# Where the causal mask of a state-space stage is added: by TensorE in PSUM, or by VectorE in the subtraction that follows

## The chip, the core and the metric

The kernel runs on one core of a Trainium2 chip. The metric is the device time of one execution in microseconds (us). Lower is better. The core has five engines that run their own instruction streams and meet at semaphores: TensorE (PE, matrix products from SBUF into PSUM), VectorE (DVE), ScalarE (ACT), GpSimd (POOL), and SyncE (SP), which here issues the transfers of the weights.

## What is computed

Two stacks of two layers each, on 512 tokens of width 1024 in fp32. The layers of the second stack have three branches: a Mamba-2 state-space branch, sliding-window attention and forgetting attention. The change lies in the first. Its core in the reference, for each of 16 heads (4 groups of 4) and each of 4 chunks of 128 tokens:

```
a_cum = jnp.cumsum(a_dt, axis=-1)
causal = idx[:, None] >= idx[None, :]
seg = a_cum[..., :, None] - a_cum[..., None, :]
decay = jnp.where(causal, jnp.exp(jnp.where(causal, seg, 0.0)), 0.0)
cb = jnp.einsum('bclgn,bcsgn->bgcls', cc, bc)
y_diag = jnp.einsum('bgrcls,bcsgrp->bclgrp', cb[:, :, None] * decay, x_dt)
...
y_off = jnp.einsum('bclgn,bcgrpn,bgrcl->bclgrp', cc, prev, jnp.exp(a_cum))
return (y_diag + y_off)
```

The kernel gets the zeros of `decay` by adding -1e30 above the diagonal (`NEG` in `consts()`) before the exponential.

## The kernel before

Weights come in 264 waves of 1 MB. SyncE loads a wave into one of two buffers, GpSimd splits it into a high and a low fp32r part (`split_wave`, L320 and L325), and TensorE makes three products for each of its tiles (high by high, low by high, high by low: L357, L358, L359 in `tile_product`). Activations are split in the same way. Nearly all TensorE time goes into these products.

No scheduler orders the work. Each engine's stream is written out by hand, and engines wait for counts of named semaphores (`s("seg")`, `s("decayed")`, ...). An engine stands at a wait until it is met, with all that is behind it.

The state-space stage is `ssm(g, first)` on TensorE and the loop over `GROUPS` (4) on VectorE and ScalarE, in each of the two layers of the second stack: 8 rounds. One group is 4 heads, r = 0 to 3. Its last part, for which these names stand:

- `rows(r)`, TensorE: a matmul L704 spreads the cumulated log-decays of head r over all partitions, 512 columns (4 chunks of 128), into bank 4 + r % 2; then four matmuls L706 of the identity with the mask add the mask to each chunk of 128 columns. The last one counts up `seg`.
- `segments(r)`, VectorE: L1745 subtracts the column of head r (its log-decays down the partitions, one value for each partition and chunk), from PSUM into `dm` (printed as merged), and counts up `seg_read`.
- ScalarE: L1155 takes the exponential of `dm` in place, and counts up `seg_exp`.
- `decay(r)`, VectorE: L1754 multiplies by `cbs`, the products of C and B, and counts up `decayed`.
- `within(r)`, TensorE: four matmuls L718 with x. `across(t)`: L724, the part from the states of earlier chunks, for two heads at a time.
- `output(t)`, VectorE: L1758, L1760 and L1762 put both parts together and count up `y_read`.
- `fill(n)`, TensorE: n times three products of the group's last waves, put between the rest so that TensorE has work while the others are busy.

The order on the two engines that matter:

```
TensorE: rows(0) rows(1) fill(6) within(0) rows(2) fill(3) within(1) across(0) rows(3) fill(4) within(2) within(3) across(1) fill(1)
VectorE: segments(0) segments(1) decay(0) segments(2) decay(1) L1772 output(0) segments(3) decay(2) decay(3) output(1)
```

`rows(r)` for r of 2 and 3 waits until `segments(r - 2)` has read the bank. `segments(r)` for r of 2 and 3 waits for `within(r - 2)`, since `dm` has two halves. `within(2)` also waits for `output(0)`, which reads the bank it writes. Ahead of `segments(0)` VectorE builds the states (L1729, L1734, L1736) from TensorE's L695.

`own` (class `Steps`) is a semaphore with which VectorE waits for its own operations: `own(ins)` counts one, `own.done()` waits until all that were counted have ended. At the start of the program VectorE casts the identity and the mask to fp32r (L1418, L1420), and TensorE waits for both (`s_setup`) ahead of the first attention heads.

Of the kernel before, what the change touches and what calls it, by code (L numbers as in the profile page):

```python
# [22 lines left out]
F32R = mybir.dt.float32r  # L23
I32 = mybir.dt.int32
ALU = mybir.AluOpType
# [3 lines left out]
P = 128  # L29
# [4 lines left out]
QB = S // P  # L34
# [23 lines left out]
C_MT, C_WM1, C_WM2 = 464, 592, 1104  # L58
# [91 lines left out]
def program(nc, weights, par1, par2, const, x_in, out, NWAVES=NWAVES):  # L150
    ctx = ExitStack()
    with ctx:
        def sb(name, shape, dt=F32, stack=ctx):
            return stack.enter_context(nc.sbuf_tensor(name, shape, dt))

        def sem(name):
            return ctx.enter_context(nc.semaphore(name))

        psum = ctx.enter_context(nc.psum_tensor("banks", [P, 8, S], F32))

        def bank(n, m=1):
            return psum[:, n:n + m, :] if m > 1 else psum[:, n, :]
# [12 lines left out]
        cst = sb("cst", [P, C_MT])  # L175
        rot = sb("rot", [P, 2, S])
        par = sb("par", [P, 160])
        identr = sb("identr", [P, P], F32R)
        seg_mask = sb("seg_mask", [P, P], F32R)
        wide_mask = sb("wide_mask", [P, C_C1 - C_WM2])  # L180
        nsink = sb("nsink", [P, 64])
        rstd = sb("rstd", [P, 16])
# [2 lines left out]
        ident = cst[:, C_ID:C_ID + P]  # L185
# [9 lines left out]
        ylo = sb("ylo", [P, KT, S], F32R, big)  # L195
        merged = sb("merged", [P, KT, S], F32, big)
        sg = sb("sg", [P, KT, S], F32, big)
        mask_in = sg[:, 0, 0:P]
        t1 = ExitStack()
        pb = [sb(f"pb{i}", [P, 2, 16 + S], F32, t1) for i in range(3)]  # L200
        pfix = sb("pfix", [P, 2, 16], F32, t1)
# [17 lines left out]
        cum = sb("cum", [P, 2, S], F32R, second)  # L219
        sel = sb("sel", [P, 4, P], F32R, second)  # L220
        selp = sb("selp", [P, 2 * P], F32R, second)
        cols = sb("cols", [P, 2, QB, 16], F32, second)
# [32 lines left out]
        dm = merged[:, 6:8, :]  # L255
# [7 lines left out]

        s_x, s_const = sem("s_x"), sem("s_const")
        s_masks, s_tables = sem("s_masks"), sem("s_tables")
        s_setup = sem("s_setup")
        s_par = sem("s_par")
        s_par_free = sem("s_par_free")
        raw_full = [sem(f"raw_full{i}") for i in range(2)]
# [7 lines left out]
        def s(name):  # L277
            if name not in sems:
                sems[name] = sem(name)
            return sems[name]  # L280
# [11 lines left out]
        @block.sync  # L292
        def _(sp):
            sp.dma_start(x[:, :, :], x_in).then_inc(s_x, 16)
            sp.dma_start(cst[:, :], const[:, 0:C_MT]).then_inc(s_const, 16)
            sp.dma_start(mask_in, const[:, C_MT:C_WM1]).then_inc(s_masks, 16)
            for p in range(2):
                sp.dma_start(raw[p][:, :], weights[p]).then_inc(raw_full[p], 16)
            sp.dma_start(rot[:, :, :], const[:, C_C1:C_C2].rearrange("p (a n) -> p a n", a=2)).then_inc(s_tables, 16)
            sp.dma_start(wide_mask[:, 0:S], const[:, C_WM1:C_WM2]).then_inc(s_tables, 16)  # L300
            with sp.Fori(1, NWAVES // 2) as j:
                for p in range(2):

                    sp.wait_ge(split, 2 * j + p - 1)
                    sp.dma_start(raw[p][:, :], weights[2 * j + p]).then_inc(raw_full[p], 16)
            sp.wait_ge(s("x_done"), 1)
            sp.dma_start(out, merged[:, :, :]).then_inc(s("stored"), 16)
            sp.wait_ge(s("stored"), 16)
# [35 lines left out]
        def _(pe):  # L344
# [104 lines left out]
            with pe.Fori(0, DEPTH) as L:  # L449
# [7 lines left out]
                for g in range(4):  # L457
# [3 lines left out]
                    for f in range(2):  # L461
                        mm = tile_product(bank(4 + 2 * (g % 2) + f), 0, g * 4 + f * 2, yhi, ylo, (2 * g, 2 * g + 1))
                    mm.then_inc(s("pool_done"), 1)
                pe.wait_ge(s("pool_read"), 4 * L + 4)
                mm = pe.matmul(psum[:, 4, 0:2], ones, lamc[:, 0:2], start=True, stop=True)
                mm.then_inc(wave_done, 1)

                pe.wait_ge(s_setup, 2)

                def tail(it, step):  # L470
                    if step == 0:
# [143 lines left out]
            with pe.Fori(0, DEPTH) as L:  # L615
                base = L * N2 + DEPTH * N1
                norm_spread(L + 2 * DEPTH)
                for p in range(2):

                    start_wave(base + p, p)  # L620
                    for k in range(KT):
                        if p == 0:
                            normed(L + 2 * DEPTH)(k)
                        mm = tile_product(bank(2 * p), p, k, xhi, xlo, [k], start=k == 0, stop=k == KT - 1)
# [27 lines left out]
                def ssm(g, first):  # L652
                    it = L * GROUPS + g
                    n = base + 4 * g + W_SSM
# [18 lines left out]
                    for t in range(3):  # L673
                        if t:
                            mm = fill((3, 5)[t - 1])
# [3 lines left out]
                        for c in range(QB):  # L679
                            mm = pe.transpose(psum[:, 7 - t, c * P:(c + 1) * P], cv[:, t, c * P:(c + 1) * P], ident)  # L680
                        mm.then_inc(s("ssm_turned"), 1)
                    pe.wait_ge(s("conv"), 4 * it + 4)
                    for c in range(QB):
                        mm = pe.matmul(psum[:, 4, c * P:(c + 1) * P], cv[:, 2, c * P:(c + 1) * P], cv[:, 3, c * P:(c + 1) * P],
                                       start=True, stop=True)
# [4 lines left out]
                    for t in range(2):  # L690
                        mm = pe.matmul(bank(4 + t), selp[:, t * P:(t + 1) * P], cum[:, 0, :], start=True, stop=True)
                    mm.then_inc(s("decay_rows"), 1)
                    pe.wait_ge(s("xdt"), it + 1)
                    for c in range(3):
                        mm = pe.matmul(psum[:, 6 + c // 2, (c % 2) * 256:(c % 2) * 256 + 256], btok[:, c, :], xd2[:, c, :],  # L695
                                       start=True, stop=True)
                    mm.then_inc(s("states"), 1)

                    def rows(r):
                        if r == 0:  # L700
                            pe.wait_ge(s("decay_out"), it + 1)
                        if r >= 2:
                            pe.wait_ge(s("seg_read"), 4 * it + r - 1)
                        pe.matmul(bank(4 + r % 2), sel[:, r, :], cum[:, 0, :], start=True, stop=False)  # L704
                        for c in range(QB):
                            mm = pe.matmul(psum[:, 4 + r % 2, c * P:(c + 1) * P], identr[:, :], seg_mask[:, :],  # L706
                                           start=False, stop=c == QB - 1)
                        mm.then_inc(s("seg"), 1)

                    def within(r):  # L710
                        if r == 0:
# [10 lines left out]
                    def across(t):  # L722
# [3 lines left out]
                        mm.then_inc(s("y_across"), 1)  # L726

                    rows(0)
                    rows(1)
                    fill(6)  # L730
                    within(0)
# [114 lines left out]
                for k in range(SWA_STEPS):  # L846
                    g, m = divmod(k, SWA_PAIRS)
# [3 lines left out]
                    def fill(first, last):  # L851
                        for i in SWA_FILL[k]:
                            cs = [c for j, c in products[first:last] if j == i]
                            if cs:
                                swa_fill(i, cs[0], cs[-1] + 1)
# [108 lines left out]
                for k in range(STEPS):  # L964
                    g, m = divmod(k, PAIRS)
# [386 lines left out]
        def _(dve):  # L1352
            own = Steps(dve, dve_own, apart)
# [61 lines left out]
            for i in range(4):  # L1415
                add_squares(0, i, IN_ORDER)
            dve.wait_ge(s_const, 16)
            dve.tensor_copy(identr[:, :], ident).then_inc(s_setup, 1)  # L1418
            dve.wait_ge(s_masks, 16)
            dve.tensor_copy(seg_mask[:, :], mask_in).then_inc(s_setup, 1)  # L1420
            with dve.Fori(0, DEPTH) as L:
                base = L * N1
                dve.wait_ge(s_par, 16 * (L + 1))
# [35 lines left out]
                for g in range(4):  # L1459
# [7 lines left out]
                    for t in range(2):  # L1467
                        c = P_PS + 2 * g + t
# [140 lines left out]
            with dve.Fori(0, DEPTH) as L:  # L1609
# [63 lines left out]
                with dve.Fori(0, GROUPS) as g:  # L1673
                    it = L * GROUPS + g
                    n = base + 4 * g + W_SSM
# [65 lines left out]
                    def segments(r):  # L1741
                        dve.wait_ge(s("seg"), 4 * it + r + 1)
                        if r >= 2:
                            dve.wait_ge(s("y_within"), 4 * it + r - 1)
                        dve.tensor_tensor(dm[:, r % 2, :].rearrange("p (c n) -> p c n", c=QB),  # L1745
                                          psum[:, 4 + r % 2, :].rearrange("p (c n) -> p c n", c=QB),
                                          cols[:, 1, :, bass.ds(4 * g + r, 1)].to_broadcast([P, QB, P]),
                                          ALU.subtract).then_inc(s("seg_read"), 1)

                    def decay(r):  # L1750
                        dve.wait_ge(s("seg_exp"), 4 * it + r + 1)
# [129 lines left out]
                for k in range(SWA_STEPS):  # L1881
                    g, m = divmod(k, SWA_PAIRS)
# [66 lines left out]
                for k in range(STEPS):  # L1949
                    g, m = divmod(k, PAIRS)  # L1950
# [220 lines left out]
```

## Time and profile before

| | |
|---|---|
| median of 3 timed runs | 3625.15 us (3624.57 to 3625.71) |
| profiled execution, its own time | 3621.37 us |
| its span, first to last instruction | 3619.5 us |
| TensorE busy, granted clock | 3457.3 us (96%), 0.983 |
| VectorE, ScalarE, GpSimd busy | 1471.9 (41%), 816.5 (23%), 2124.9 us (59%) |
| mask matmuls L706 | 128 in all |
| `segments` L1745 | 32, of 688 ns |

The profile is one execution as the hardware profiler recorded it. Times within it count from its first instruction. A matmul's record lasts longer than the time for which it holds TensorE (the pipeline overlaps the next one: wave products of 390 ns start 0.23 us apart), so what a matmul costs is read from the distance of two starts, or from the chain of waits, where the pieces follow each other without overlap. "L12" is line 12 of the kernel before. An engine name with a q (DVEq) is that engine's queue of small instructions: address computations and waits.

### The profile page before, as it was taken

How to read it: one execution, taken by the hardware profiler on the slowest of the kernel's cores; microseconds unless marked ns; L12 is line 12 of the kernel's file. 1: busy time of each engine (PE TensorE's matmuls, PEld its weight loads, DVE VectorE, ACT ScalarE, POOL GpSimd, SP SyncE). 2: the span in 40 equal slices, each digit the busy share in tenths (PEclk: the TensorE clock that was granted, in tenths of full speed). 3: DMA queues.
4: the chain of work that ended last, by engine and by line, in shares of the span. 5: the costliest groups of instructions: out<-in, count | busy, mean ns of one | idle time of the engine just before them, and what ended most of it. 6: DMA issues, size and time to landing. Idle time of an engine off the chain costs nothing.

```text
span 3619.5 us, 49401 instructions
## 1 busy us (share of the span) xinstructions
PE 3457.3 (96%) x17270; PEld 2766.4 (76%) x17270; DVE 1471.9 (41%) x2814; ACT 816.5 (23%) x1659; POOL 2124.9 (59%) x2116
## 2 busy tenths in 40 slices
PE   8999899998999899999999999999899999999998
PEld 6778688887777688877877777777778777777776
DVE  4545322104555321116664652332366545523323
ACT  1223111001233111002222540332122225413320
POOL 6745567766555477665556556445756475464454
PEclk9999999999999999999999999999999999999998
DMA  3211122222211122231212212111212122121121
GB/s 129 83 68 70 62 88 94 93 101 75 82 62 66 70 93 93 94 115 59 81 68 83 71 70 94 60 70 70 95 68 74 68 84 79 72 82 70 59 70 70
DMA packets 39930, 285.38 MB, mean 79 GB/s; under 512 B 4688, under 2 KB 5200, under 8 KB 5728
## 3 DMA queue, kind: packets, MB, share of 16 engines
q1 hardware_dynamic: 38880, 282.13, 21.5%
q8 instruction: 104, 1.70, 0.2%
q10 hardware_dynamic: 896, 1.14, 0.1%
q14 instruction: 50, 0.41, 0.0%
HBM read 281.15 MB, written 2.10 MB: 78 GB/s over the span
## 4 chain that ended last, share of the span: by engine, by line
PE 83%; DVE 8%; issue 4%; ACT 3%; POOL 1%; DMA 0%; DVEq 0%; ACTq 0%; POOLq 0%
PE banks L357 20%; PE banks L359 19%; PE banks L358 19%; PE banks L596 2%; PE banks L595 2%; PE banks L594 2%; PE banks L909 1%; PE banks L933 1%; PE banks L920 1%; PE banks L400 1%; PE banks L565 1%; PE banks L402 1%; PE banks L401 1%; PE banks L912 1%; PE banks L718 1%
## 5 line engine op out<-in xcount | busy, mean ns | idle before, releaser
L320 POOL TENSOR_SCALAR whi<-raw 128x512 fp32r<-128x512 f32 x1056 | 731.5, 702 | 1457.6 <-PE banks L359 1223.4
L325 POOL TENSOR_TENSOR wlo<-raw,whi 128x512 fp32r<-128x512 f32 x1056 | 1438.1, 1372 | 0.0
L357 PE MATMUL banks<-xhi,whi 128*128 128x512 f32 x2976 | 1220.6, 410 | 41.3 <-DVE xlo L1387 15.4
L359 PE MATMUL banks<-xhi,wlo 128*128 128x512 f32 x2976 | 1169.7, 393 | 0.0
L358 PE MATMUL banks<-xlo,whi 128*128 128x512 f32 x2976 | 1167.6, 392 | 0.0
L357 PEld LDWEIGHTS banks<-xhi,whi 128*128 128x128 f32 x2976 | 564.2, 190 | 190.0 <-issue 33.3
L359 PEld LDWEIGHTS banks<-xhi,wlo 128*128 128x128 f32 x2976 | 562.9, 189 | 123.9
L358 PEld LDWEIGHTS banks<-xlo,whi 128*128 128x128 f32 x2976 | 565.1, 190 | 109.6 <-issue 6.7
L357 PE MATMUL banks<-yhi,whi 128*128 128x512 f32 x544 | 217.5, 400 | 17.0 <-DVE ylo L1557 5.6
L358 PE MATMUL banks<-ylo,whi 128*128 128x512 f32 x544 | 214.0, 393 | 0.0
L359 PE MATMUL banks<-yhi,wlo 128*128 128x512 f32 x544 | 213.7, 393 | 0.0
L1919 DVE CUSTOM_DVE_ANT_0 banks<-banks,wide_mask 128x128 f32<-128x128 f32 (+3 forms) x128 | 63.4, 495 | 262.9 <-PE banks L912 262.9
L1585 DVE SCALAR_TENSOR_TENSOR hg<-hg,banks 128x512 f32<-128x512 f32 x44 | 30.2, 687 | 335.2 <-ACT hg L1094 335.2
L1294 ACT ACTIVATE work<-banks,st 128x128 f32<-128x128 f32 (+3 forms) x128 | 67.5, 528 | 322.7 <-PE banks L920 320.9
L594 PE MATMUL banks<-hhi,whi 128*128 (+1 forms) x352 | 136.9, 389 | 0.0
L595 PE MATMUL banks<-hlo,whi 128*128 (+1 forms) x352 | 136.9, 389 | 0.0
L596 PE MATMUL banks<-hhi,wlo 128*128 (+1 forms) x352 | 136.9, 389 | 0.0
L357 PEld LDWEIGHTS banks<-yhi,whi 128*128 128x128 f32 x544 | 103.5, 190 | 43.7 <-issue 8.9
L359 PEld LDWEIGHTS banks<-yhi,wlo 128*128 128x128 f32 x544 | 103.4, 190 | 22.0
L358 PEld LDWEIGHTS banks<-ylo,whi 128*128 128x128 f32 x544 | 103.3, 190 | 22.0 <-issue 1.0
L1094 ACT ACTIVATE hg<-banks 128x512 f32<-128x512 f32 x44 | 26.4, 599 | 348.2 <-PE banks L359 348.2
L1008 ACT ACTIVATE merged<-x 128x1024 f32<-128x1024 f32 x24 | 25.1, 1058 | 349.3 <-DVE x L1599 233.5
(260 smaller groups left out, 4260.0 us busy)
## 6 DMA issues: line engine op xcount, KB each, us to landing
raw<-weights SPq DMA_DIRECT2D x264, 1024.0 KB, 4.8
x<-x_in SPq DMA_DIRECT2D x1, 2048.0 KB, 8.2
out<-merged SPq DMA_DIRECT2D x1, 2048.0 KB, 6.3
rot<-const SPq DMA_DIRECT2D x1, 512.0 KB, 11.8
rot<-const ACTq DMA_DIRECT2D x1, 512.0 KB, 3.3
wide_mask<-const ACTq DMA_DIRECT2D x1, 384.0 KB, 4.1
wide_mask<-const SPq DMA_DIRECT2D x1, 256.0 KB, 12.5
cst<-const SPq DMA_DIRECT2D x1, 232.0 KB, 8.4
```

The source lines that it names most:

```text
L320: pool.tensor_scalar(whi[p][:, w], raw[p][:, w], 1.0, 1.0, ALU.mult, ALU.mult).then_inc(s("hi_written"), 1)
L325: return pool.tensor_tensor(wlo[p][:, w], raw[p][:, w], whi[p][:, w].bitcast(F32), ALU.subtract)
L357: pe.matmul(dst, whi[p][:, w], hi[:, k, :], start=start and i == 0, stop=False)
L358: pe.matmul(dst, whi[p][:, w], lo[:, k, :], start=False, stop=False)
L359: mm = pe.matmul(dst, wlo[p][:, w], hi[:, k, :], start=False, stop=stop and last_k)
L400: pe.matmul(dst, xhi[:, k, t], whi[p][:, w], start=k == 0, stop=False)
L401: pe.matmul(dst, xlo[:, k, t], whi[p][:, w], start=False, stop=False)
L594: pe.matmul(bank(f), whi[p][:, w], hhi[:, k0 + k2, :], start=start and k2 == 0, stop=False)
L595: pe.matmul(bank(f), whi[p][:, w], hlo[:, k0 + k2, :], start=False, stop=False)
L596: mm = pe.matmul(bank(f), wlo[p][:, w], hhi[:, k0 + k2, :], start=False, stop=stop and k2 == 1)
L1294: act.activation(pr2[:, u % 2, 0:w], psum[:, 4 + u % 3, 0:w], ACT.Exp, scale=-1.0, bias=st2[:, 1, c:c + 1], accum_out=st2[:, 2, c:c + 1]). ...
L1919: dve.tensor_tensor_reduce(sc, sc, blocked(w), -0.125, FAR, ALU.add, ALU.min, st2[:, 1, c:c + 1]).then_inc(s("fox_max"), 1)
```

## The change

TensorE's four identity matmuls of each `rows(r)` go, and `seg` is counted up by the spreading matmul. VectorE's one subtraction over 128x512 becomes four scalar_tensor_tensor over 128x128, one for each chunk: (PSUM - column) + mask, with the column as a [128, 1] scalar and the mask from SBUF. The first three are counted by `own`; the fourth waits for them and counts up `seg_read`. The mask stays in fp32 and is loaded straight to its place, the fp32r copy of the identity goes, and so do the two casts at the start and TensorE's wait for them.

```diff
-        identr = sb("identr", [P, P], F32R)
-        seg_mask = sb("seg_mask", [P, P], F32R)
+        seg_mask = sb("seg_mask", [P, P])
...
-        mask_in = sg[:, 0, 0:P]
...
-        s_setup = sem("s_setup")
...
-            sp.dma_start(mask_in, const[:, C_MT:C_WM1]).then_inc(s_masks, 16)
+            sp.dma_start(seg_mask[:, :], const[:, C_MT:C_WM1]).then_inc(s_masks, 16)
...
-                pe.wait_ge(s_setup, 2)
...
-                        pe.matmul(bank(4 + r % 2), sel[:, r, :], cum[:, 0, :], start=True, stop=False)
-                        for c in range(QB):
-                            mm = pe.matmul(psum[:, 4 + r % 2, c * P:(c + 1) * P], identr[:, :], seg_mask[:, :],
-                                           start=False, stop=c == QB - 1)
-                        mm.then_inc(s("seg"), 1)
+                        pe.matmul(bank(4 + r % 2), sel[:, r, :], cum[:, 0, :], start=True, stop=True).then_inc(s("seg"), 1)
...
             dve.wait_ge(s_const, 16)
-            dve.tensor_copy(identr[:, :], ident).then_inc(s_setup, 1)
             dve.wait_ge(s_masks, 16)
-            dve.tensor_copy(seg_mask[:, :], mask_in).then_inc(s_setup, 1)
...
-                        dve.tensor_tensor(dm[:, r % 2, :].rearrange("p (c n) -> p c n", c=QB),
-                                          psum[:, 4 + r % 2, :].rearrange("p (c n) -> p c n", c=QB),
-                                          cols[:, 1, :, bass.ds(4 * g + r, 1)].to_broadcast([P, QB, P]),
-                                          ALU.subtract).then_inc(s("seg_read"), 1)
+                        for c in range(QB):
+                            if c == QB - 1:
+                                own.done()
+                            ins = dve.scalar_tensor_tensor(dm[:, r % 2, c * P:(c + 1) * P], psum[:, 4 + r % 2, c * P:(c + 1) * P],
+                                                           cols[:, 1, c, bass.ds(4 * g + r, 1)], seg_mask[:, :],
+                                                           ALU.subtract, ALU.add)
+                            if c < QB - 1:
+                                own(ins)
+                            else:
+                                ins.then_inc(s("seg_read"), 1)
```

VectorE's stream from the last step of the states to `decay(0)`, before (ISA rows are queue instructions, here the computation of an address; merged is `dm`):

```order
L1734 TENSOR_TENSOR hst<-hst,banks 128x256 [waits dve_own]
L1745 ISA [waits dve_own,seg]
L1745 TENSOR_TENSOR merged<-banks,cols 128x512
L1745 ISA [waits seg]
L1745 TENSOR_TENSOR merged<-banks,cols 128x512
L1753 ISA [waits seg_exp]
L1754 TENSOR_TENSOR merged<-merged,cbs 128x512 [waits ssm_evac]
```

and now, where `segments` is L1738 and `decay` L1750; of the two `segments` the second stands here:

```order
L1738 ISA [waits seg]
L1738 SCALAR_TENSOR_TENSOR merged<-banks,cols,seg_mask 128x128
L1738 ISA
L1738 SCALAR_TENSOR_TENSOR merged<-banks,cols,seg_mask 128x128
L1738 ISA
L1738 SCALAR_TENSOR_TENSOR merged<-banks,cols,seg_mask 128x128
L1738 ISA [waits dve_own]
L1738 SCALAR_TENSOR_TENSOR merged<-banks,cols,seg_mask 128x128
L1749 ISA [waits seg_exp]
L1750 TENSOR_TENSOR merged<-merged,cbs 128x512 [waits ssm_evac]
```

The order of the steps is the same. Each of the four operations has its own address instruction, and that of the fourth stands behind the wait for the first three.

## Rows read from the trace of the kernel before

**Rows 1.** The page: busy time of the engines; shares of the chain that ended last.
```profile
PE 3457.3 (96%) x17270; PEld 2766.4 (76%) x17270; DVE 1471.9 (41%) x2814; ACT 816.5 (23%) x1659; POOL 2124.9 (59%) x2116
...
PE 83%; DVE 8%; issue 4%; ACT 3%; POOL 1%; DMA 0%; DVEq 0%; ACTq 0%; POOLq 0%
```

**Rows 2.** Chain of waits in the second group, `rows(0)`: start us, us, what.
```profile
1751.77 0.32 PE banks L704
1752.08 0.40 PE banks L706 x4
```

**Rows 3.** The same chain, from `across(0)` to `within(2)`.
```profile
1762.30 0.88 PE banks L724 x6
...
1763.21 0.06 DVEq L1758
...
1763.32 0.75 DVE ya L1758
...
1764.54 0.02 issue
...
1765.45 0.69 DVE merged L1745
...
1766.76 0.14 issue
1766.89 1.79 PE banks L718 x16
```

**Rows 4.** Who TensorE waited for: us in total, times, longest.
```profile
PE banks L718 <- DVE merged L1754: 2.3, 8, 0.3
```

**Rows 5.** Timeline of VectorE, second group: start us, us, instruction [idle before <-releaser].
```profile
1754.02 0.42 DVE L1734 TENSOR_TENSOR hst<-hst,banks 128x256 f32<-128x256 f32 x1
1754.69 1.29 DVE L1745 TENSOR_TENSOR merged<-banks,cols 128x512 f32<-128x512 f32 x2 [0.26 <-DVE hst L1734]
1756.18 0.69 DVE L1754 TENSOR_TENSOR merged<-merged,cbs 128x512 f32<-128x512 f32 x1 [0.21 <-ACT merged L1155]
1759.32 0.69 DVE L1745 TENSOR_TENSOR merged<-banks,cols 128x512 f32<-128x512 f32 x1 [2.45 <-PE banks L706]
1759.93 0.68 DVE L1754 TENSOR_TENSOR merged<-merged,cbs 128x512 f32<-128x512 f32 x1
...
1763.32 0.75 DVE L1758 SCALAR_TENSOR_TENSOR ya<-merged,par,banks 128x512 f32<-128x512 f32 x1 [1.58 <-PE banks L724]
1763.98 0.55 DVE L1760 TENSOR_TENSOR ea<-ea,banks 128x384 f32<-128x384 f32 x1
```

**Rows 6.** Timeline of TensorE, second group: `within(0)` and `within(1)`.
```profile
1757.26 1.09 PE L718 MATMUL banks<-merged 128*64 128x128 f32 x8
...
1761.21 1.09 PE L718 MATMUL banks<-merged 128*64 128x128 f32 x8
```

**Rows 7.** Groups of VectorE instructions by shape: busy us, mean ns | idle before.
```profile
L1919 DVE CUSTOM_DVE_ANT_0 banks<-banks,wide_mask 128x512 f32<-128x512 f32 x32 | 22.3, 696 | 60.5 <-PE banks L912 60.5
...
L1758 DVE SCALAR_TENSOR_TENSOR ya<-merged,par,banks 128x512 f32<-128x512 f32 x16 | 12.0, 747 | 29.9 <-PE banks L724 29.9
L1837 DVE CUSTOM_DVE_ANT_0 banks<-banks,wide_mask,nsink 128x128 f32<-128x128 f32 x32 | 11.5, 359 | 36.3 <-PE banks L803 28.2 <-DVE work L1850 7.4 <-DVE st L1837 0.8
...
L1919 DVE CUSTOM_DVE_ANT_0 banks<-banks,wide_mask 128x128 f32<-128x128 f32 x32 | 9.5, 296 | 97.5 <-PE banks L912 97.5
...
L1516 DVE CUSTOM_DVE_ANT_0 banks<-banks,wide_mask,rqs 128x128 f32<-128x128 f32 x16 | 5.5, 359 | 6.4 <-PE banks L533 6.4
```

**Rows 8.** Timeline of VectorE at the program's start, the first operation behind the casts.
```profile
17.88 0.17 DVE L1359 TENSOR_SCALAR banks<-banks 128x4 f32<-128x4 f32 x1 [2.44 <-PE banks L419]
```

**Rows 9.** Timeline of TensorE, two gaps in later stages.
```profile
1942.36 0.47 PE L357 MATMUL banks<-xhi,whi 128*128 128x512 f32 x1 [1.68 <-DVEq L1806]
...
1982.76 0.87 PE L814 MATMUL banks<-cst,work 128*128 128x128 f32 x3 [2.03 <-ACT work L1190]
```

**Rows 10.** Stretches around these gaps: us, PE busy (x), granted clock, DMA share, GB/s.
```profile
1982.80:1986.20 3.40, 3.40 (x11) 0.51 0.57 241
...
1940.00:1946.00 6.00, 4.33 (x20) 1.00 0.36 152
```

## The prediction

> **What bounds the kernel now.** I read the page first. TensorE is busy 96% of the span and holds 83% of the chain that ended last, VectorE 8% [rows 1]: as a whole TensorE is the bound, VectorE has spare time, and the change seems to move work from the full engine to one at 41%. That average says nothing of the stage that changes, so the sum is made there. The stage runs 8 times (4 groups in each of 2 layers). I read the chain of waits in the second group, then VectorE's and ScalarE's timelines there, and at last the prices of small VectorE operations.
>
> The chain shows that `rows` costs 0.32 + 0.40 us, 0.40 us of it the four mask matmuls of 128 columns [rows 2]. It also shows where TensorE does not set the pace: between `across(0)` and `within(2)` it runs through VectorE, from the end of L724 at 1763.18 through L1758, L1760, L1762, `segments(3)` (L1745) and `decay(2)` (L1754) to the matmuls L718 at 1766.89 [rows 3]. TensorE waits for L1754 in all 8 groups alike, 2.3 us in total and 0.3 at most [rows 4]. The other two hand-overs are nearly tight. The multiply of `decay(0)` starts at 1756.18 and that of `decay(1)` at 1759.93, 0.69 and 0.68 us long [rows 5]; with 0.14 us to the matmul [rows 3] they would release `within(0)` at 1757.01 and `within(1)` at 1760.75. TensorE reaches these at 1757.26 and 1761.21 (its L718 in [rows 6]). The slack is 0.25 and 0.46 us.
>
> **The removed matmuls.** 8 groups x 4 rows x 0.40 = 12.8 us of TensorE time. It counts only where no wait takes its place. `rows(0)` and `rows(1)` lie before `within(0)`, `rows(2)` before `within(1)`, and `rows(3)` runs beside the VectorE chain of [rows 3], so its 0.40 turns into waiting at once. Even if VectorE paid nothing more, `within(0)` could come only 0.25 earlier, since `decay(0)` waits for the exponential of `segments(0)`, which starts when VectorE has the states (L1734 ends 1754.44, L1745 starts 1754.69 [rows 5]). `within(1)` would then gain its 0.40, `within(2)` nothing: 0.65 us a group, **5.2 us at most** in all.
>
> **The price of four small operations.** Let T be the time from the start of a `segments` to the start of the operation behind it; now 0.61 (1759.32 to 1759.93 [rows 5]). The new form is four scalar_tensor_tensor of 128x128, from PSUM and `seg_mask`, with the column as a pointer scalar. No such row exists. The nearest is the custom operation of L1837 and L1516 (PSUM, an SBUF mask and a pointer scalar, 128x128): 359 ns. Without a pointer (L1919) it is 296, and at 512 columns 696; so 384 columns are worth 0.40 us and a pointer 0.06 [rows 7]. Scalar_tensor_tensor with a pointer takes 747 at 512 (L1758) [rows 7], less 0.40 is 0.35: I take **0.35**. It releases the engine earlier than it ends: L1758 starts at 1763.32, the next at 1763.98 [rows 5], 0.66, less 0.40 is **0.26**. The fourth waits until the third has ended and then computes its address: from L724's end at 1763.18 to L1758, the same pair of steps, 0.14 [rows 3]; its bounds are 0.02, a wait with no address (the issue between L1760 and L1762, rows 3), and 0.26, with one more queue step (L1734 to L1745, rows 5). So T = 0.26 + 0.26 + 0.35 + 0.14 + 0.26 = **1.27**. The low bound is the price without a pointer: 0.20 + 0.20 + 0.30 + 0.02 + 0.20 = 0.92. The high one lets nothing overlap and takes 359: 4 x 0.36 + 0.26 = 1.70. By the sum below these ends are worth 0 and 23.9 us. The addresses of the second and third (0.06 each on the queue, as for L1758 in rows 3) fit under 0.26.
>
> The Trainium skill (VectorE: DVE Perf Modes, The TRN2 errata) gives PSUM to SBUF 120 cycles plus one per column at 0.96 GHz, 258 ns at 128 columns. As an estimate by that page, with the overlap of 0.09 and the wait of 0.14, T would be 0.17 + 0.17 + 0.26 + 0.14 + 0.17 = 0.91 and the change free. The trace disagrees for operands like these: 296 without and 359 with a pointer.
>
> **The sum**, in the second group's times. 1: `decay(0)` stands behind two `segments`: 1754.69 + 2T = 1757.23 (the exponential no longer decides: from the end of the first L1745 at 1755.38 to L1754 at 1756.18 it took 0.80 [rows 5], so it would allow 1754.69 + 1.36 + 0.80 = 1756.85). Plus 0.69 and 0.14: `within(0)` at 1758.06 instead of 1757.26, **+0.80**; TensorE was there at 1756.46 and idles. 2: `segments(2)` waits for `rows(2)`, which follows `within(0)`; it came 2.06 after it (1759.32 less 1757.26), now 0.40 earlier, 1.66. Then T, 0.69, 0.14: `within(1)` 3.76 behind `within(0)`, where it was 3.95: **-0.19**. TensorE alone could do 3.55. 3: up to `within(2)` the chain of [rows 3] is longer by T - 0.61: **+0.66**. 4: `decay(3)` and `within(3)` keep their distances, because both ends of that hand-over slide with `segments(3)`. VectorE's L1772, which stands between, was over before L1758 with 1.58 us to spare (its idle time in [rows 5]), and now follows `decay(1)` as before, which slides by 1.06 while L1758 slides by 0.61: 1.13 us are left. Together 1.27 us a group, in general 4T - 3.81. Times 8: **+10.2 us**. Behind `across(1)` the distances stay and nothing absorbs the delay: TensorE goes on with wave products at its own pace.
>
> **The start.** The two casts go; behind them VectorE waits 2.44 us for TensorE's L419 [rows 8], so they are worth 0. TensorE's wait for them, ahead of the first attention heads, is worth 0 too: they ended before 17.88. The mask's DMA goes to another place, with the same bytes: 0. It makes 3621.4 + 10.2 = 3631.6 for the profiled execution. The median of the timed runs stands 3.8 above it; the same 10.2 on 3625.15 gives **3635.4 us**. About 0.2%, 7.25 us, is what a measurement of this kernel can tell from no change; T has to exceed 1.18 for that.
>
> **The rivals.** A, cheap small operations, the other side: with the 296 of L1919, intervals of 0.20 and 0.14 for the wait, T = 1.04. Below 1.06 TensorE sets `within(1)` itself, and a group costs 3T - 2.75 = 0.37: **3628.2**, no difference; it turns to a gain below T = 0.92. For it: L1745 reads the same column, as a tensor, and takes no more (0.69 [rows 5]) than L1919 at 512 without a pointer (696 [rows 7]). Against it: every scalar pointer in rows 7 costs 0.06. B, nothing overlaps: T = 3 x 0.35 + 0.14 + 0.35 = 1.54, 2.35 us a group, **3644**. Against it: L1745 starts twice in 1.29 us at 0.69 each [rows 5], an overlap of 0.09. The Trainium skill (VectorE: DVE Perf Modes, The DRAIN you can't avoid) says that the next operation does not start before the pipe is empty; that is this rival, and that row speaks against it. C, the clock: TensorE now stands idle 1.6 us before `within(0)` and 0.28 + 0.66 + 0.40 = 1.3 before `within(2)`. A gap of 1.68 left the granted clock at 1.00; one of 2.03 was followed by 3.4 us at 0.51 [rows 9, 10], 1.2 GHz for 2.4, which costs 1.7 us. If it fell in one of the two places in each group, 13.6 more: **3649**. D, the matmuls' time counts in full, as on an engine that bounds everything: 12.8 less, **3612**. Against it stands the wait of [rows 4] and the bound of 5.2.
>
> **How the numbers follow.** Forecast (T from 1.18 to 1.4) 0.58; A with all T up to 1.18, 0.27; B 0.06; C 0.07; D 0.02. Slower by over 0.2%: 0.58 + 0.06 + 0.07 = 0.71; within: 0.27; faster: 0.02. The range runs from just under A's 3628.2 to 3642.5, T = 1.4 and a few falls of the clock; B, D, most of C and the lowest T stay out, under 0.2.
>
> **What would show it.** TensorE's matmuls 12.8 us less, and its waits for the `decay` line from 2.3 to about 24 us, nearly all before `within(0)` and `within(2)`; VectorE busy some 20 us more; new operations of 0.35 us, 0.26 apart with a fourth 0.49 behind the third; `segments(0)` to `decay(0)` 2.5 us where it was 1.49. Wrong: small operations at 0.30 or less, no wait at `within(0)`, a granted clock below 1.00 in the stage, or a distance from one group's `segments(0)` to the next group's that is not 1.3 us longer.

## The result and the profile after

The change makes the kernel slower by a third of a per cent: 3633.82 us median (8 runs, 3631.58 to 3639.96) against 3623.41 (8 runs, 3620.22 to 3625.71), 10.4 us. The ratio is 1.0033, 95% interval 1.0022 to 1.0044. Forecast were 10.2 us more, 3635.4 us.

The page of the changed kernel, busy times and shares of the chain, against [rows 1]:

```profile
span 3632.0 us, 49336 instructions
...
PE 3444.2 (95%) x17142; PEld 2752.5 (76%) x17142; DVE 1489.5 (41%) x2908; ACT 816.8 (22%) x1659; POOL 2125.2 (59%) x2116
...
PE 81%; DVE 10%; issue 4%; ACT 3%; POOL 1%; DMA 0%; DVEq 0%; ACTq 0%; POOLq 0%
```

TensorE is busy 13.1 us less and VectorE 17.6 us more. TensorE got its relief; the span grew by 12.5 us all the same. Where it went stands in the waits of TensorE (who waited for whom: us in total, times, longest), against [rows 4]:

```profile
PE banks L710 <- DVE merged L1750: 24.8, 16, 1.7
```

L710 is `within`, L1750 `decay`. The wait was 2.3 us, 8 times; it is 24.8 us, 16 times. The timeline of VectorE in the second group (the counterpart of [rows 5]; L1738 is the new `segments`):

```profile
1755.80 0.42 DVE L1724 TENSOR_TENSOR hst<-hst,banks 128x256 f32<-128x256 f32 x1
1756.49 2.63 DVE L1738 SCALAR_TENSOR_TENSOR merged<-banks,cols,seg_mask 128x128 f32<-128x128 f32 x8 [0.26 <-DVE hst L1724]
1759.04 0.68 DVE L1750 TENSOR_TENSOR merged<-merged,cbs 128x512 f32<-128x512 f32 x1
1761.50 1.36 DVE L1738 SCALAR_TENSOR_TENSOR merged<-banks,cols,seg_mask 128x128 f32<-128x128 f32 x4 [1.78 <-PE banks L700]
1762.78 0.68 DVE L1750 TENSOR_TENSOR merged<-merged,cbs 128x512 f32<-128x512 f32 x1
...
1767.75 1.36 DVE L1738 SCALAR_TENSOR_TENSOR merged<-banks,cols,seg_mask 128x128 f32<-128x128 f32 x4 [0.33 <-DVE ya L1758]
1769.03 1.47 DVE L1750 TENSOR_TENSOR merged<-merged,cbs 128x512 f32<-128x512 f32 x2
```

T, the time from a `segments` to what is behind it, is 1.28 us (1761.50 to 1762.78); 1.27 was forecast and 0.61 it was. `decay(0)` starts 2.55 us behind `segments(0)` (1756.49 to 1759.04), where it was 1.49. TensorE in the same group, against [rows 6]:

```profile
1759.87 1.06 PE L710 MATMUL banks<-merged 128*64 128x128 f32 x8 [1.69 <-DVE merged L1750]
...
1763.52 1.09 PE L710 MATMUL banks<-merged 128*64 128x128 f32 x8
...
1769.86 1.35 PE L710 MATMUL banks<-merged 128*64 128x128 f32 x12 [1.41 <-DVE merged L1750]
```

These are `within(0)`, `within(1)` and `within(2)`. Two waits, 1.69 and 1.41 us, where there was one of 0.28. The chain of waits shows what a `segments` consists of (start us, us, what):

```profile
1767.65 0.06 DVEq L1738
1767.70 0.05 issue
1767.75 0.08 DVE merged L1738
1767.83 0.07 issue
1767.90 0.06 DVEq L1738
1767.96 0.06 issue
1768.02 0.61 DVE merged L1738 x2
1768.63 0.03 issue
1768.66 0.06 DVEq L1738
1768.71 0.05 issue
1768.76 0.35 DVE merged L1738
1769.12 0.61 DVE merged L1750
1769.72 0.14 issue
1769.86 1.24 PE banks L710 x11
```

First to second operation 0.27 us, the third at 0.26 more, and the fourth 0.14 behind the end of the third: the wait (0.03), the address (0.06) and the issue (0.05) that the prediction took from [rows 3]. The operation itself, by shape:

```profile
L1738 DVE SCALAR_TENSOR_TENSOR merged<-banks,cols,seg_mask 128x128 f32<-128x128 f32 x128 | 38.3, 346 | 23.7 <-PE banks L700 14.3 <-DVE ya L1758 2.7 <-DVE hst L1724 2.1
```

346 ns, against 0.35 forecast.

The profiled execution took 12.4 us more than that of before (12.5 by the span), and the stage explains 9.6 of it: the length of a group, measured from one group's L695 to the next one's, went from 58.42 to 59.62 us. The rest lies outside: 0.6 us ahead of the first group, 0.6 between the layers, 1.7 behind the last group. In the last part the granted clock fell once more than before, at 3013.8:

```profile
3013.80:3017.20 3.40, 3.40 (x11) 2.73 (x12) 2.59 (x12) 0.00 (x0) 0.00 (x0) 0.52 0.16 65
```

(columns: stretch, us, busy us of PE, PEld, DVE, ACT and POOL with counts, granted clock, DMA share, GB/s). This fall lost 1.6 us. Between the layers it is the other way round: the kernel before has a fall there (0.66 from 2640 to 2645, 1.7 us) that the changed one does not have. So the clock does not account for the 2.9 us outside the stage, and where they come from stays open. This is why the experiments below are read by the length of a group and confirmed by the timed runs.

### The profile page after: what moved, and what is told of

Same layout as the page of the kernel before. It is cut to its first block, busy times and chain, and to the rows that moved or that the text cites. A ratio compares the mean times of both kernels' runs of the same rounds, so it can differ in the third digit from the quotient of the medians.

```text
span 3632.0 us, 49336 instructions
## 1 busy us (share of the span) xinstructions
PE 3444.2 (95%) x17142; PEld 2752.5 (76%) x17142; DVE 1489.5 (41%) x2908; ACT 816.8 (22%) x1659; POOL 2125.2 (59%) x2116
## 4 chain that ended last, share of the span: by engine, by line
PE 81%; DVE 10%; issue 4%; ACT 3%; POOL 1%; DMA 0%; DVEq 0%; ACTq 0%; POOLq 0%
PE banks L354 19%; PE banks L356 19%; PE banks L355 19%; PE banks L592 2%; PE banks L591 2%; PE banks L590 2%; PE banks L901 1%; PE banks L925 1%; PE banks L912 1%; PE banks L397 1%; PE banks L561 1%; PE banks L399 1%; PE banks L398 1%; PE banks L710 1%; PE banks L904 1%
## 6 DMA issues: line engine op xcount, KB each, us to landing
wide_mask<-const SPq DMA_DIRECT2D x1, 256.0 KB, 12.4
```

## The experiments

The theory: in this stage TensorE is released at three places by VectorE, and T decides when. The rivals: the removed matmuls' time counts in full; the loss comes from elsewhere (the start, moved addresses); or it is spread evenly over the heads. The table has what the traces of all kernels show in the second group, in us: `within(0)` from the group's first L695, the two distances that follow, and the length of a group (mean of the second and third, first layer). The second layer agrees within 0.05. Single groups stay within 0.1 of these means too, but for the three kernels whose group is marked with a star: there the granted clock fell in some groups and not in others, and the mean has both (below).

| kernel | within(0) | to within(1) | to within(2) | group | timed median, and before beside it |
|---|---|---|---|---|---|
| before | 6.95 | 3.95 | 5.68 | 58.42 | |
| the change | 7.78 | 3.65 | 6.34 | 59.62 | 3633.82 / 3623.41 |
| e1_no_mask | 6.71 | 3.52 | 5.68 | 57.71 | 3615.36 / 3622.34 |
| e2_no_own_wait | 7.31 | 3.48 | 6.10 | 58.73 | 3626.58 / 3622.34 |
| e3_head3_only | 6.95 | 3.95 | 6.36 | 59.10 | 3626.88 / 3622.34 |
| e4_head2_only | 6.95 | 3.69 | 5.67 | 58.17 | 3620.87 / 3622.34 |
| e5_heads01_only | 7.79 | 3.93 | 5.67 | 59.24 | one run, 3630.08 / 3624.33 |
| e6_decay0_first | 7.39 | 3.66 | 6.34 | 59.23 | one run, 3627.56 / 3624.33 |
| e11_casts_kept | 7.79 | 3.65 | 6.35 | 59.60 | one run, 3634.04 / 3624.33 |
| e9_fill_alone | 7.62 | 3.95 | 6.01 | 61.58* | 3645.35 / 3622.60 |
| e10_after_fill | 8.22 | 3.65 | 6.35 | 61.27* | 3647.92 / 3622.60 |
| e7_wide_mask | 6.72 | 3.72 | 5.68 | 57.96 | 3619.29 / 3622.60 |
| e8_wide_mask_fill | 7.17 | 3.74 | 5.75 | 59.98* | 3634.89 / 3622.60 |
| e12_wide_mask_fill2 | 6.72 | 3.23 | 5.76 | 57.44 | 3614.37 / 3622.05 |

### Taking the matmuls away for nothing

```diff
 # before, with
-                        pe.matmul(bank(4 + r % 2), sel[:, r, :], cum[:, 0, :], start=True, stop=False)
-                        for c in range(QB):
-                            mm = pe.matmul(... identr[:, :], seg_mask[:, :] ...)
-                        mm.then_inc(s("seg"), 1)
+                        pe.matmul(bank(4 + r % 2), sel[:, r, :], cum[:, 0, :], start=True, stop=True).then_inc(s("seg"), 1)
...
-                        act.activation(dm[:, r % 2, :], dm[:, r % 2, :], ACT.Exp).then_inc(s("seg_exp"), 1)
+                        act.activation(dm[:, r % 2, :], dm[:, r % 2, :], ACT.Exp, scale=0.001).then_inc(s("seg_exp"), 1)
```

> The kernel before without the mask matmuls, and with VectorE's one wide subtraction; the mask is left out of the computation, and the exponent is scaled by 0.001 so that it stays finite. Waits theory: TensorE has 1.60 us a group less to do, but decay(0) still waits for the states and the exponential, and within(2) for the VectorE chain, so a group gets only 0.65 us shorter (58.43 to about 57.8) and the kernel 5.2 us faster than before. TensorE-bound rival: the matmuls' time counts in full, 1.60 a group, 12.8 us faster.

Measured: a group 0.71 us shorter, and 3615.36 against 3622.34 us (ratio 0.9980, 0.9971 to 0.9989). VectorE's timeline in the second group:

```profile
1754.80 1.29 DVE L1741 TENSOR_TENSOR merged<-banks,cols 128x512 f32<-128x512 f32 x2 [0.26 <-DVE hst L1730]
1756.29 0.69 DVE L1750 TENSOR_TENSOR merged<-merged,cbs 128x512 f32<-128x512 f32 x1 [0.21 <-ACT merged L1151]
```

`decay(0)` stands 1.49 us behind `segments(0)`, exactly as before [rows 5]: TensorE's 0.80 us ahead of it gained only the 0.24 of slack. The saving is capped at 0.7 of 1.6 us a group even when VectorE pays nothing. By the groups that is 5.7 us in all; the timed 7.0 has an interval of about 4 to 10.5, which holds 5.7 and excludes 12.8.

### Making the four operations shorter

```diff
-                            if c == QB - 1:
-                                own.done()
-                            ins = dve.scalar_tensor_tensor(...)
-                            if c < QB - 1:
-                                own(ins)
-                            else:
-                                ins.then_inc(s("seg_read"), 1)
+                            dve.scalar_tensor_tensor(...).then_inc(s("seg_read"), 1)
...
-    pe.wait_ge(s("seg_read"), 4 * it + r - 1)
+    pe.wait_ge(s("seg_read"), 16 * it + 4 * r - 4)
...
-    act.wait_ge(s("seg_read"), 4 * it + r + 1)
+    act.wait_ge(s("seg_read"), 16 * it + 4 * r + 4)
```

> The changed kernel, but all four operations of a segments count up seg_read and the readers wait for four counts, so the fourth does not wait for the third. T falls from 1.28 to 4 x 0.26 = 1.04. Waits theory: a group costs 0.3 to 0.4 us more than before instead of 1.17 (58.8 against 59.6), the kernel 2 to 3 us more than before, some 7 us less than with the change. Rival, the loss does not come from the length of segments (start of the program, moved addresses, the removed matmuls' place): as the change, 59.6 and +10 us.

Measured: a group of 58.73 us, 0.31 above before and 0.89 below the change; 3626.58 against 3622.34 us (ratio 1.0011, 1.0002 to 1.0020). The same operations, in VectorE's timeline:

```profile
1759.78 1.13 DVE L1736 SCALAR_TENSOR_TENSOR merged<-banks,cols,seg_mask 128x128 f32<-128x128 f32 x4 [1.78 <-PE banks L700]
1760.83 0.68 DVE L1744 TENSOR_TENSOR merged<-merged,cbs 128x512 f32<-128x512 f32 x1
```

T is 1.05. VectorE computes the same as with the change, so the 0.23 us by which T is shorter is the one wait of the fourth operation for the third, and it carried three quarters of the change's loss (0.89 of 1.20 a group). The length of `segments` is what costs, not the place of the mask.

### One head at a time

Heads that keep the form of before keep both their mask matmuls and the wide subtraction:

```diff
+                        if r in (3,):      # (2,) and (0, 1) in the other two
+                            pe.matmul(... start=True, stop=True).then_inc(s("seg"), 1)
+                        else:
                             ...
```

> The kernel before, with the change's form in head 3 alone (heads 0 to 2 keep their mask matmuls). Waits theory: rows(3) runs beside the VectorE chain, so its 0.40 us saved is worth nothing and the longer segments(3) comes on top: within(2) 0.66 us later, a group of 59.1 us, +5.3 us against before: more than half of the loss from a quarter of the change. Even rival, each head carries a quarter: +0.29 a group, +2.4 us. TensorE-bound rival: -0.40 a group, -3.2 us.

> The kernel before, with the change's form in head 2 alone. Waits theory: within(1) had 0.46 us of slack; TensorE arrives 0.40 earlier and the product 0.67 later less 0.40, so within(1) comes 0.2 to 0.3 us earlier: a group of 58.1 to 58.2 us and 1.5 to 2.4 us less than before, a gain. Even rival: +0.29 a group, +2.4 us.

> The kernel before, with the change's form in heads 0 and 1 alone. Waits theory: within(0) comes 0.83 later, as with the change, and everything behind keeps its distance: a group of 59.2 us, +6.6 us. With head 2 (-0.25) and head 3 (+0.70) alone it should add up to the change's +1.21: 0.83 - 0.25 + 0.70 = 1.28. Even rival: +0.60 a group. TensorE-bound rival: -0.80.

Measured: head 3 alone +0.68 us a group and 4.5 us by the timed medians (ratio 1.0012, 1.0002 to 1.0021); head 2 alone -0.25 and -1.5 us (0.9994, 0.9985 to 1.0003, so the gain is shown by the trace only); heads 0 and 1 +0.82, by its trace and one run. Together 1.25, where the change has 1.20. The even rival fell: the same four operations cost 0.7 us in one head and give back a quarter in the next. In `e3_head3_only` the timeline of VectorE has the long `segments` at one place only:

```profile
1763.61 0.69 DVE L1760 TENSOR_TENSOR merged<-banks,cols 128x512 f32<-128x512 f32 x1 [2.44 <-PE banks L709]
...
1769.75 1.36 DVE L1752 SCALAR_TENSOR_TENSOR merged<-banks,cols,seg_mask 128x128 f32<-128x128 f32 x4 [0.34 <-DVE ya L1777]
```

and TensorE's waits there are

```profile
PE banks L721 <- DVE merged L1769: 11.3, 8, 1.4
```

where [rows 4] had 2.3: +9.0 us, of which 3.2 are the matmuls' saved time that turned into waiting, and 5.4 the longer group; 0.4 is left over.

### Another order of the same work

```diff
                     segments(0)
+                    decay(0)
                     segments(1)
-                    decay(0)
```

> The changed kernel with decay(0) ahead of segments(1) on VectorE. The same operations, another order. Waits theory: decay(0) then waits for the exponential of segments(0) (1.36 + 0.80 behind its start) instead of for two segments (2.55): within(0) 0.39 us earlier, the rest at its distance, a group of 59.2 instead of 59.6 us, 3 us less than with the change. Rival, VectorE's amount of work decides and not what stands ahead of decay(0): no difference.

Measured: `within(0)` at 7.39 instead of 7.78, a group 0.39 us shorter, as expected. VectorE:

```profile
1755.99 1.36 DVE L1738 SCALAR_TENSOR_TENSOR merged<-banks,cols,seg_mask 128x128 f32<-128x128 f32 x4 [0.27 <-DVE hst L1724]
1758.15 0.69 DVE L1750 TENSOR_TENSOR merged<-merged,cbs 128x512 f32<-128x512 f32 x1 [0.80 <-ACT merged L1147]
1758.76 1.36 DVE L1738 SCALAR_TENSOR_TENSOR merged<-banks,cols,seg_mask 128x128 f32<-128x128 f32 x4
```

VectorE now stands idle 0.80 us for the exponential, and the kernel is still faster than with the change: what stands ahead of `decay(0)` counts, not how much VectorE does.

### The start of the program

```diff
 # the change, with the fp32r mask, the casts and the wait kept:
+            dve.tensor_copy(identr[:, :], ident).then_inc(s_setup, 1)
+            dve.tensor_copy(seg_mask[:, :], mask_in).then_inc(s_setup, 1)
...
+                pe.wait_ge(s_setup, 2)
```

> The changed kernel with the two casts at the start, the fp32r mask and TensorE's wait for them kept. They are hidden: group of 59.6 us as with the change, first norm operation of VectorE at 17.9 us as before. Rival, start or addresses carry a part: another length of the group or a start that is 1 to 2 us later.

Measured: 59.60 us a group, the change's 59.62. Of VectorE's first operation behind the casts, the changed kernel's timeline stands first, that of this kernel second:

```profile
17.84 0.17 DVE L1351 TENSOR_SCALAR banks<-banks 128x4 f32<-128x4 f32 x1 [4.24 <-PE banks L416]
```

```profile
17.81 0.17 DVE L1355 TENSOR_SCALAR banks<-banks 128x4 f32<-128x4 f32 x1 [2.43 <-PE banks L419]
```

Without the casts VectorE only waits longer. They were worth 0.

### Filling the waits: a theory that held in one part and fell in another

If TensorE waits, wave products could stand there. The first attempt moved two of them, in the kernel before and in the changed one:

```diff
-                    fill(2)                       # ahead of the decay rows
+                    fill(1)
...
-                    fill(6)                       # ahead of within(0)
+                    fill(7)
...
-                    fill(4)                       # ahead of within(2)
+                    fill(5).then_inc(wave_done, 1)
                     within(2)
                     within(3)
                     across(1)
-                    fill(1).then_inc(wave_done, 1)
```

> The kernel before (mask matmuls kept) with the fill moved: fill(2) to fill(1) ahead of the decay rows, fill(6) to fill(7) ahead of within(0), fill(4) to fill(5) ahead of within(2), and none behind across(1). Waits theory: only the 0.44 us of waiting at within(2) can be filled: a group 0.35 to 0.45 us shorter, 58.0 us, 3 us less than before. Rival, TensorE is busy all the time in this stage and order is worth nothing: no difference.

> The changed kernel with the same move of the fill. Waits theory: both waits (1.6 us before within(0), 1.4 before within(2)) take a product of 0.68 us each without getting longer, so a group loses 1.2 to 1.3 us: 58.4 us, the change's whole loss comes back and it stands level with before (within 1 us), but behind the same move without the change. Rival, the loss is VectorE's work as such: stays near +10.

Measured: `e9_fill_alone` is 22.8 us slower than before (ratio 1.0061, 1.0047 to 1.0075) where 3 us less were expected, and `e10_after_fill` 25.3 us slower (1.0069, 1.0055 to 1.0083) where no difference was. The group of `e9_fill_alone` is 3.16 us longer. The trace names a hand-over that the theory had left out: TensorE's L411, the sums for the group's norm, in the next group's first wave.

```profile
PE banks L411 <- DVE merged L1784: 20.9, 8, 5.6
```

Before, TensorE waited for this operation in the last group of each layer only (two waits, 7.5 us together). Now it also waits 1.60 us in each of the other six. In the second group of `e9_fill_alone`, VectorE's tail and TensorE's wait:

```profile
1776.82 1.15 DVE L1761 TENSOR_TENSOR ya<-ya,ea 128x384 f32<-128x384 f32 x1
...
1780.78 1.66 DVE L1784 TENSOR_TENSOR merged<-merged 128x512 f32<-128x512 f32 x1 [1.27 <-ACT merged L1161]
```

```profile
1782.49 1.05 PE L411 MATMUL banks<-cst,merged 128*128 128x1 f32 x8 [1.60 <-DVE merged L1784]
```

```profile
1782.50:1790.00 7.50, 7.50 (x30) 6.14 (x31) 2.52 (x12) 0.00 (x0) 0.00 (x0) 0.77 0.39 140
```

The same two VectorE operations took 0.56 and 1.01 us before:

```profile
1770.94 0.56 DVE L1762 TENSOR_TENSOR ya<-ya,ea 128x384 f32<-128x384 f32 x1
...
1774.32 1.01 DVE L1785 TENSOR_TENSOR merged<-merged 128x512 f32<-128x512 f32 x1 [1.27 <-ACT merged L1162]
```

What GpSimd does at that time, first in `e9_fill_alone` and then before (its split of the next wave begins with L320):

```profile
1773.27 1.20 POOL L320 TENSOR_SCALAR whi<-raw 128x512 fp32r<-128x512 f32 x2 [12.62 <-PE banks L359]
```

```profile
1770.47 1.51 POOL L320 TENSOR_SCALAR whi<-raw 128x512 fp32r<-128x512 f32 x2 [15.33 <-PE banks L359]
```

Three things come together. The product that stood behind `across(1)` had covered VectorE's tail, and is gone. The wave ends earlier, so that GpSimd begins to split the next one 2.3 us ahead of this tail (1773.27, the tail's first operation 1775.57), where before it began 0.8 us behind the tail's start (1770.47 and 1769.70). GpSimd works beside the tail in both kernels, but on other steps of the split, and the tail is 1.24 us longer. And behind the gap of 1.60 us, which is followed by eight matmuls of one column, the granted clock falls: 0.77 over 7.5 us is 3.4 us at 1.2 GHz, 1.7 us lost.

The clock fell behind five of these six gaps (1.60 or 1.61 us). The first of them had no fall, and its group is 59.92 us long; the next two are 61.60 and 61.57. In `e8_wide_mask_fill`, below, it fell behind four of six such gaps (groups of 60.79, 59.17 and 60.79 us), and in `e10_after_fill`, where these gaps are 1.02 to 1.06 us, behind two of six (60.48, 62.07, 60.46). So the length of the gap alone doesn't tell whether the clock falls.

By the second group, the moved products gained 0.35, as forecast for them; 1.6 went for the wait and 1.7 for the clock, and 0.2 is left over. That the shifted split is what slows the two operations rests on their timing, since no kernel moved the split alone.

> The kernel before with the mask twice side by side, so that two identity matmuls of 256 columns add it instead of four of 128. rows costs about 0.23 instead of 0.40 us more than the spreading matmul, if 256 columns cost 0.12. VectorE unchanged. Waits theory: within(0) 0.25 earlier at most, within(1) 0.17, within(2) nothing: a group of 58.0 us, 3.4 us less than before. TensorE-bound rival: 4 x 0.17 a group, 5.4 us less.

> Both: two mask matmuls of 256 columns and the moved fill. Waits theory: 0.34 at within(0) (the states come earlier too), 0.17 at within(1), 0.3 to 0.4 at within(2) and behind it: a group of 57.4 us, 8 us less than before and less than either alone.

```diff
-        seg_mask = sb("seg_mask", [P, P], F32R)
+        seg_mask = sb("seg_mask", [P, 2 * P], F32R)
...
-                        for c in range(QB):
-                            mm = pe.matmul(psum[:, 4 + r % 2, c * P:(c + 1) * P], identr[:, :], seg_mask[:, :],
-                                           start=False, stop=c == QB - 1)
+                        for c in range(2):
+                            mm = pe.matmul(psum[:, 4 + r % 2, c * 2 * P:(c + 1) * 2 * P], identr[:, :], seg_mask[:, :],
+                                           start=False, stop=c == 1)
```

The pair of wide matmuls costs 0.25 instead of 0.40 us, in the chain of waits of `e7_wide_mask`:

```profile
1752.94 0.32 PE banks L704
1753.27 0.25 PE banks L706 x2
```

A group is 0.46 us shorter (0.42 expected), 3619.29 against 3622.60 us (0.9989, 0.9980 to 0.9998). With the moved fill on top (`e8_wide_mask_fill`) it is 12.3 us slower than before (1.0032, 1.0020 to 1.0045), where 8 us less were expected. TensorE waits 20.9 us for the norm sums at L411 as in `e9_fill_alone`, with the falls of the clock counted above; that expectation missed in the same way.

The last kernel tests the explanation: the same wide mask, one product moved from in front of `within(1)`, and everything behind `across(1)` left alone.

```diff
 # e7_wide_mask, and
                     rows(2)
-                    fill(3)
+                    fill(2)
                     within(1)
...
                     rows(3)
-                    fill(4)
+                    fill(5)
                     within(2)
```

> Two mask matmuls of 256 columns as in e7_wide_mask, and one product of the fill moved from fill(3), ahead of within(1), to fill(5), ahead of within(2); fill(1) stays behind across(1) and no wave ends earlier. Waits theory: within(0) 0.24 earlier as in e7_wide_mask; within(1) then follows 3.33 behind it, set by VectorE, instead of 3.72; within(2) follows at 5.7 to 5.8, because TensorE now fills its wait there: a group of 57.6 to 57.7 us, 6 us less than before. Since GpSimd's split starts where it did, VectorE's tail is not slowed, TensorE does not wait at the norm sums (L411), and the clock stays at 1.00 in the stage. Rival, any move of the fill costs as in e9_fill_alone: +20 us.

Measured: a group of 57.44 us, 0.98 shorter than before (0.2 more than expected, 0.10 of it at `within(1)`), and 3614.37 against 3622.05 us: ratio 0.9978, 0.9969 to 0.9987. TensorE's wait at `within` is gone from the list, L411 is back at twice 3.7, and the clock stays at 1.00 in the stage. GpSimd's split begins 0.8 us behind the tail's start again (1768.97 and 1768.20), and the two operations of the tail take 0.56 and 1.01 us. The waits of TensorE and the stretch of the first layer's groups:

```profile
PE banks L411 <- DVE merged L1786: 7.5, 2, 3.7
```

```profile
1690.00:1886.00 196.00, 194.04 (x982) 158.11 (x981) 128.51 (x212) 45.11 (x62) 107.28 (x107) 1.00 0.20 70
```

This version is 7.7 us faster than the kernel before, and so faster than the change. It keeps the mask on TensorE.

## Why the prediction was right

**The bound.** The step that decided the sign held: the engine that is busy 96% of the span is not the one that sets the pace at these three hand-overs. The cap on the saving was 0.65 us a group; 0.71 was measured without any mask.

**The removed matmuls.** 12.8 us of TensorE time were forecast to go, and 13.1 went from its busy time. TensorE's wait for the `decay` line grew by 22.5 us: that is the 13.1, all of which turned into waiting, and the 9.6 by which the groups are longer, within 0.2.

**The price.** Operation 0.35 (346 ns), interval 0.26 (0.26 to 0.27), the fourth behind the third 0.14 (0.14), T 1.27 (1.28). The row with a pointer scalar was the right neighbour. Rival A (296 ns, as without a pointer) fell. With it fell the estimate by the Trainium skill (VectorE: DVE Perf Modes, The TRN2 errata): 258 ns, where the trace has 346. Rival B, no overlap, fell too: the operations stand 0.26 apart at 0.34 to 0.35 each. The section that the prediction names beside this rival (the Trainium skill, VectorE: DVE Perf Modes, The DRAIN you can't avoid) goes on to say that a next operation that is not held starts earlier, so it does not stand for rival B, and the trace agrees with it.

**The sum.** `within(0)` +0.83 (forecast +0.80), to `within(1)` -0.30 (-0.19), to `within(2)` +0.66 (+0.66): 1.19, and 1.20 by the length of a group, against 1.27. The one term that was off is the second. `within(1)` starts 0.06 us behind `decay(1)` (the issue of 0.04 in the chain of waits, not 0.14), and the wide spread without mask matmuls releases VectorE a little sooner. In the code `within(1)` waits for one semaphore and the other two for a pair of them; that this makes the difference is not shown. Times 8 it is 9.6 us of the measured 10.4. The remaining 0.8 is within what the runs scatter (the interval of the ratio is about 8 to 16 us). That 10.2 came so near to 10.4 is therefore partly luck: the stage alone was forecast 0.6 us too high. In the prediction's text rival A's 0.37 us a group gives 3628.1 us and not 3628.2, which changes nothing.

**The waits.** About 24 us forecast for TensorE at `decay`, 24.8 measured, before `within(0)` and `within(2)` as said.

**The clock, rival C.** The granted clock stayed at 1.00 behind the gaps of 1.69 and 1.41 us in the stage, so it cost nothing there. It was no safe bet: ahead of L411 in the moved-fill kernels the clock fell behind five of six gaps of 1.60 us, and behind two of six of 1.02 to 1.06. What parts these from the gaps in the stage is not shown; what follows them differs, eight matmuls of one column there and 128 columns here.

**What the prediction did not have** is the fourth hand-over, at L411. It did not matter for the change, which shifts both of its sides alike, and it sank the first attempt at a better version.

## What to carry to other kernels

Work taken off the fullest engine pays only where that engine is not waiting for the one that takes it over. Find the hand-overs in the stage, write down the slack of each, and put the new length of the receiving operations into them; here 1.6 us of saved time a group became 1.2 us of loss. When one wide operation is cut into four, price the pieces by a row with the same kind of operands, and count the wait that joins them: 0.23 us of it was three quarters of the loss. Before moving cover work, look at what it covers in the next step as well.

## What the runs showed of the hardware that was not expected

- A [128, 1] scalar from SBUF adds 0.06 us to a VectorE operation, at 128 columns (the same custom operation took 359 against 296 ns) as at 512 (scalar_tensor_tensor 747 against 687 ns at L1585). Scalar_tensor_tensor operations with it of 128 columns start 0.26 us apart: four take 1.05 us where one of 512 takes 0.61.
- An fp32r matmul of 256 columns costs TensorE 0.12 us, one of 128 columns 0.10 (0.25 for two and 0.40 for four in the chain of waits): widening the mask was nearly free.
- Two VectorE operations on SBUF operands took 0.56 and 1.01 us, and 1.15 and 1.66 in the kernel in which GpSimd's split of a wave began 3.1 us earlier against them. The new operations kept 340 to 353 ns, but GpSimd stood idle beside nearly all of them.
- The granted clock fell behind some gaps of TensorE of 1.02 to 1.06 us and not behind others of 1.69; where it fell in the stage, a group was 1.6 to 1.7 us longer.
